# Six short vectors loaded as rows and spread by a product with ones, and the other small loads split over two semaphores

## What is computed

```
h = rms_norm(x, norm1_g)
proj = h @ w_in                                  # 1024 x 2856, read in six pieces
q = rms_norm(q, nsa_q_norm_g)                    # per head of 64
kc = rms_norm(silu(blocks(k_c) @ cmp_w1_k) @ cmp_w2_k, nsa_k_norm_g[0])
ks = rope(rms_norm(k_s, nsa_k_norm_g[1]));  kw = rope(rms_norm(k_w, nsa_k_norm_g[2]))
...                                              # attention branches, gated linear attention
o = rms_norm(o_gla, gla_norm_g) * silu(r)
x = x + concat(nsa, gla) @ w_out
logits = rms_norm(x, norm2_g) @ w_router + b_router
x = x + sum over the top 4 of 32 experts of gate * expert(x)   # w_gate_up, w_down: 32 x 12 MB
```

## Time and profile before

| | |
|---|---|
| median of 3 runs | 1162.44 us (1160.12 to 1165.05) |
| the profiled execution's own time | 1164.05 us |
| its span, first to last instruction | 1162.0 us |
| PE busy | 1083.2 us, 93% |
| DVE, ACT, POOL busy | 275.6, 129.9, 17.2 us |
| DMA moved | 426.37 MB, 367 GB/s on average |
| software DMA queue q0 | 752 packets, 1.32 MB, 1.3% of 16 engines' time |

### The profile page before, as it was taken

One profiled execution on the slowest core, in us unless ns is written; L12 is line 12 of the kernel. 1 busy time (PEld: TensorE's weight loads), 2 busy tenths in 40 slices (PEclk: granted clock), 3 DMA queues, 4 the chain that ended last, 5 costly groups with the idle time before them and its releaser, 6 DMA issues.

```text
span 1162.0 us, 13609 instructions
## 1 busy us (share of the span) xinstructions
PE 1083.2 (93%) x5502; PEld 485.6 (42%) x5502; DVE 275.6 (24%) x660; ACT 129.9 (11%) x290; POOL 17.2 (1%) x45
## 2 busy tenths in 40 slices
PE   7789999999999999999999999999999999999997
PEld 5354555444444443344333334334343433333442
DVE  1255442322222222222222111112222211221222
ACT  2224313000000000000000000000000000000001
POOL 5000000000000000000000000000000000000000
PEclk9889989999999999999999999999999999999999
DMA  9941253699999999999999999999999999999996
GB/s 210 336 157 73 73 218 144 259 399 418 418 418 418 418 419 418 418 417 417 418 417 418 417 418 417 419 417 418 417 418 418 417 418 418 418 418 419 418 418 277
DMA packets 83471, 426.37 MB, mean 367 GB/s; under 512 B 4752, under 2 KB 9968, under 8 KB 50656
## 3 DMA queue, kind: packets, MB, share of 16 engines
q1 hardware_dynamic: 82704, 424.85, 90.2%
q0 software_dynamic: 752, 1.32, 1.3%
HBM read 425.11 MB, written 1.05 MB: 367 GB/s over the span
## 4 chain that ended last, share of the span: by engine, by line
DMA 59%; PE 36%; DVE 2%; issue 1%; POOL 1%; ACT 1%; SPq 0%; DVEq 0%; POOLq 0%; ACTq 0%
DMA stage<-in_w_gate_up 54%; PE bank L1398 16%; PE bank L1407 5%; PE bank L1075 4%; PE bank L1388 3%; PE bank L1324 3%; DMA stage<-in_w_down 2%; DMA bdn<-in_b_down 2%; PE bank L1430 1%; PE bank L1091 1%; DMA stage<-in_w_in 1%; PE bank L1131 0%; PE bank L1114 0%; DVE pb L784 0%; PE bank L1422 0%
## 5 line engine op out<-in xcount | busy, mean ns | idle before, releaser
L1398 PE MATMUL bank<-stage,xs 128*64 128x512 f32 x2048 | 457.3, 596 | 48.5 <-DMA stage<-in_w_gate_up 46.8
L1398 PEld LDWEIGHTS bank<-stage,xs 128*64 128x64 f32 x2048 | 140.0, 137 | 360.7 <-issue 269.5
L1407 PE MATMUL bank<-stage,actf 128*64 128x512 f32 x1024 | 227.0, 595 | 1.2 <-DMA stage<-in_w_down 1.2
L992 DVE COPY gu<-bank 128x512 f32<-128x512 f32 x32 | 22.1, 692 | 450.2 <-PE bank L1398 450.2
L1388 PEld LDWEIGHTS bank<-onehot,xr 128*128 128x128 f32 x1024 | 116.8, 192 | 25.6 <-issue 25.6
L1407 PEld LDWEIGHTS bank<-stage,actf 128*64 128x64 f32 x1024 | 70.6, 137 | 132.4 <-issue 121.4
L1388 PE MATMUL bank<-onehot,xr 128*128 128x64 f32 x1024 | 121.0, 276 | 0.0
L1075 PE MATMUL bank<-stage,xt 128*128 128x512 f32 (+1 forms) x192 | 87.6, 610 | 0.9 <-DVE xt L685 0.9
L594 ACT COPY gu<-bank 128x512 f32<-128x512 f32 x32 | 18.8, 586 | 473.1 <-PE bank L1398 473.1
L1430 PE MATMUL bank<-ys,pgt 64*128 64x512 f32 x256 | 63.6, 615 | 1.0 <-ACT ys L598 1.0
L1014 DVE TENSOR_TENSOR pgr<-iota_f,posm 128x256 f32<-128x256 f32 x32 | 13.6, 425 | 188.2 <-PE bank L1415 188.2
(11 more groups left out here) (285 smaller groups left out, 430.3 us busy)
## 6 DMA issues: line engine op xcount, KB each, us to landing
stage<-in_w_gate_up SPq DMA_DIRECT2D x128, 2048.0 KB, 23.9
stage<-in_w_down SPq DMA_DIRECT2D x62, 2048.0 KB, 24.0
stage<-in_w_in SPq DMA_DIRECT2D x5, 2048.0 KB, 33.4
stage<-in_w_out SPq DMA_DIRECT2D x2, 2048.0 KB, 10.4
stage<-in_w_down SPq DMA_DIRECT2D x4, 1024.0 KB, 18.8
stage<-in_cmp_w_k SPq DMA_DIRECT2D x1, 2048.0 KB, 22.9
stage<-in_cmp_w_v SPq DMA_DIRECT2D x1, 2048.0 KB, 20.8
stage<-in_w_in SPq DMA_DIRECT2D x1, 1120.0 KB, 7.5
```

The costliest lines, as they stand in the source:

```text
L992: V.tensor_copy(gu[:, 1, :], up_banks[1][:]).then_inc(s["gu_lo"], 1)
L1398: last = mm(up_banks[a][b * CAP:(b + 1) * CAP, :], xs[:, k, :], w[:, kk, FF * a + 512 * b:FF * a + 512 * (b + 1)], start=k == 0, stop=k == ...
L1407: last = mm(down_bank[b * CAP:(b + 1) * CAP, :], actf[:, kk, j, :], w[:, kk, 512 * b:512 * (b + 1)], start=j == 0 and kk == 0, stop=j == D ...
```

## The change

The six broadcast loads (three into `g12`, one each into `gk0`, `glag` and `brt`) go. Four loads put the vectors behind each other into one row, `vecs`, of 416 numbers on partition 0. After `project(3)` PE multiplies a row of ones by it (`ones[0:1, :]`, 1 x 128, times 1 x 416), so that bank 3 holds the row in all 128 partitions. Six DVE instructions copy the parts to `g12`, `gk0`, `brt` and `glag`; the last also applies the factor 0.5 that `glag` had got in an instruction of its own. PE's next use of bank 3 waits for them (`gains`). `small` now counts ten loads: `wgate`, its bias, the positions, the four rows, `brow` and the two `posl`. The seven others (`w2`, `wrt`, `bdn`) come behind them and count on a new semaphore `late`, which DVE waits for ahead of the scaling of `wrt`, and PE ahead of `gated_bias` at 227 us. The memsets of `glrt` and `ones` move ahead of the loads on POOL, and ACT's copy into `glrt` waits for three of POOL's constants, not for all 20.

```diff
-N_SMALL = 19
+N_SMALL = 10
+N_LATE = 7
...
+            step(nc.gpsimd.memset(glrt[:], 1.0))
+            step(nc.gpsimd.memset(ones[:], 1.0))
             small = [
                 (wgate[0:RANK, :], gla_w_gate[0]),
                 (wgate[RANK:RANK + 1, :], gla_b_gate[0:1, :]),
                 (poss[:], positions[0].rearrange("(t p) -> p t", p=P)),
+                (vecs[:, 0:DH], nsa_q_norm_g[0:1, :]),
+                (vecs[:, DH:4 * DH], nsa_k_norm_g.rearrange("o b d -> o (b d)")),
+                (vecs[:, 4 * DH:4 * DH + DV], gla_norm_g[0:1, :]),
+                (vecs[:, 4 * DH + DV:], b_router[0:1, :]),
                 (brow[:], b_gate_up[0]),
                 (posl[:, 0, :], cmp_pos_k[0].rearrange("(c i) d -> c (i d)", i=2)),
                 (posl[:, 1, :], cmp_pos_v[0].rearrange("(c i) d -> c (i d)", i=2)),
-                (g12[:, 0:HQ, :], nsa_q_norm_g[0:1, :].partition_broadcast(P).to_broadcast([P, HQ, DH])),
-                (g12[:, HQ:HQ + 2, :], nsa_k_norm_g[0, 1:2, :].partition_broadcast(P).to_broadcast([P, 2, DH])),
-                (g12[:, HQ + 2:HQ + 4, :], nsa_k_norm_g[0, 2:3, :].partition_broadcast(P).to_broadcast([P, 2, DH])),
-                (gk0[:], nsa_k_norm_g[0, 0, :].partition_broadcast(NCW)),
-                (glag[:], gla_norm_g[0].partition_broadcast(P)),
+            ]
+            late = [
                 (w2[:, 0, :, :], split_k(cmp_w2_k[0])),
                 (w2[:, 1, :, :], split_k(cmp_w2_v[0])),
                 (wrt[:], split_k(w_router[0])),
-                (brt[:], b_router[0].partition_broadcast(P)),
             ] + [(bdn[r * E:(r + 1) * E, :], ...) for r in range(4)]
...
-            act.wait_ge(s["const"], N_CONST)
+            act.wait_ge(s["const"], 3)
             act.wait_ge(s["glrt_full"], 1)
...
+            dve.wait_ge(s["rows_full"], 1)
+            heads = banks[3][:, 0:4 * DH].rearrange("p (b d) -> p b d", d=DH)
+            V.tensor_copy(g12[:, 0:HQ, :], heads[:, 0:1, :].to_broadcast([P, HQ, DH]))
+            for b in range(2):
+                V.tensor_copy(g12[:, HQ + 2 * b:HQ + 2 * b + 2, :], heads[:, 2 + b:3 + b, :].to_broadcast([P, 2, DH]))
+            V.tensor_copy(gk0[:], banks[3][0:NCW, DH:2 * DH])
+            V.tensor_copy(brt[:], banks[3][:, 4 * DH + DV:4 * DH + DV + E])
+            V.tensor_scalar(glag[:], banks[3][:, 4 * DH:4 * DH + DV], 0.5, None, ALU.mult).then_inc(s["gains"], 1)
+            dve.wait_ge(s["gains"], 1)
             dve.wait_ge(s["small"], 16 * N_SMALL)
...
+            dve.wait_ge(s["late"], 16 * N_LATE)
             V.tensor_tensor(wrt[:], wrt[:], bc(gt2[:, DK:2 * DK], E), ALU.mult)
-            V.tensor_scalar(w2[:], w2[:], 0.5, None, ALU.mult)
-            link(V.tensor_scalar(glag[:], glag[:], 0.5, None, ALU.mult))
+            link(V.tensor_scalar(w2[:], w2[:], 0.5, None, ALU.mult))
...
             pe.wait_ge(s["small"], 16 * N_SMALL)
+            pe.wait_ge(s["const"], 4)
+            mm(banks[3][:, 0:4 * DH + DV + E], ones[0:1, :], vecs[:], start=True, stop=True).then_inc(s["rows_full"], 1)
...
             pe.wait_ge(s["proj"], 4)
+            pe.wait_ge(s["gains"], 1)
...
+            pe.wait_ge(s["late"], 16 * N_LATE)
             gated_bias()
```

More of the change, by code:

```diff
@@ L140, in decoder_layer @@
         g12 = sb("g12", [P, 12, DH])
+        vecs = sb("vecs", [1, 4 * DH + DV + E])
         gt = sb("gt", [P, NT, 24 + RANK])
@@ L215, in decoder_layer @@
             "xin0 xin1 grows g1_full g1t xt_full xt ms_x rsx proj_full proj small const act dve rope sin "
-            "glrw glrt_full glrt bias_full bias z_full absz e1 loga b_full bexp dec qd qdt_full qdt at_full ats "
+            "late rows_full gains glrw glrt_full glrt bias_full bias z_full absz e1 loga b_full bexp dec qd qdt_full qdt at_full ats "
             "u_full sta sgr grg o_full gsq glaout kx_full kx post_full post tb h_full sigh hid ht_full hidt "
@@ L370, in _ @@
                 (wrt[:], split_k(w_router[0])),
-                (brt[:], b_router[0].partition_broadcast(P)),
             ] + [(bdn[r * E:(r + 1) * E, :], b_down[0][:, 512 * (r % 2):512 * (r % 2) + 512]) for r in range(4)]
+            assert len(small) == N_SMALL and len(late) == N_LATE
             pool.wait_ge(s["stage0"], 16)
@@ L376, in _ @@
                 pool.dma_start(dst, src, allow_slow_non_contiguous=True).then_inc(s["small"], 16)
-            assert len(small) == N_SMALL
-            step(nc.gpsimd.memset(glrt[:], 1.0))
-            step(nc.gpsimd.memset(ones[:], 1.0))
+            for dst, src in late:
+                pool.dma_start(dst, src, allow_slow_non_contiguous=True).then_inc(s["late"], 16)
             step(nc.gpsimd.memset(tri[:], 1.0))
```

## The result

The changed kernel takes 1146.61 us (median of 4, 1146.35 to 1148.58), the kernel before in the same comparison 1163.74 us (median of 4). The ratio is 0.9858, 95% interval 0.9826 to 0.9890: 17.1 us faster, where 13.1 were forecast. The time lies 2.7 us under the 1149.3 that were forecast; the other 1.3 us of the difference are the kernel before, whose median was 1163.74 here and 1162.44 in the prediction. The profiled execution took 1148.58 us, the longest of the four, with a span of 1146.8 us, 15.2 less than before. What follows accounts for these 15.2 us, and the other 1.9 of the 17.1 are in no trace.

What follows compares the result with a forecast made beforehand. Expert-loop weight loads fill over half the span and start when the front ends, so the front's gain is the kernel's. 13.3 us at `hidden(8, 16)` less 0.2 slack gives 13.1; off the 1162.44 median, 1149.3 us, range 1146.5 to 1155.0.

Steps and rivals of the forecast that it cites:

- The two waits: Front, PE: 6.0 us behind `project(3)` for `bdn`, 3.94 us at `hidden(0, 8)` for `cmp_w1_v`; both late from slow broadcast packets.
- The stream: SP's loads in the front run 12.2 us earlier (13.4 + 1.3 - 2.5); `cmp_w1_v` lands at 55.9, not 68.1.
- the price of what stays: Front, software queue: the remaining 0.79 MB of small loads cost SP's stream 2.5 us.
- Which loads: Front, 19 to 29 us: the slow packets, 1.9 us each, are those of the broadcasts.
- PE's way: PE from `project(3)` to `hidden`: `project(4)` ends at 44.5, 9.0 us earlier; PE reaches `hidden` at 55.3.
- DVE's way: `norm_heads(1)` ends 16.1 us after `project(4)`, at 60.6; PE waits; `hidden(8, 16)` ends at 64.9, gain 13.3 us.
- from there on ... everything moves by as much: After `hidden(8, 16)`: no load is late, and everything moves by the same gain, 13.1 us after slack.
- D: Rival: PE's terms at their lower ends and clock up later in the front, another 2 us: 1147, chance 0.1.
- B: Rival: broadcasts cost only their bytes, the hole is the software queue's; no change, 1162.4, chance 0.07.
- C: Rival: the `late` loads hold DVE; slower, at 65 us it would cost 8 us, 1170; chance 0.02.
- A: Rival: `cmp_w1_v`'s load decides at `hidden(0, 8)`, not DVE; stream wins only 9 us; gain 9.1, 1153.3; chance 0.17.

Runs made afterwards that it cites:

- split_only: Kernel before with the second semaphore alone, broadcasts, w2, wrt and bdn counted on `late`, plus ACT's shorter wait for POOL's constants: 1162.79 us, ratio 0.9982.
- others_back: Changed kernel plus the five smaller broadcasts (all but the q gains') as loads that nothing reads, in their old places: 1149.90 us, ratio 0.9897.
- q_one_head: Kernel before with q gains spread by DMA once per partition, not eight times, DVE copying the other seven heads: 1149.51 us, ratio 0.9907.
- rows_one_sem: Changed kernel with all 17 small loads on one semaphore again, so the split is undone: 1147.10 us, ratio 0.9865.
- stall_only: rows_one_sem with the last small load issued only when `project(3)` is done, so PE stalls without the slow stream: 1159.26 us, ratio 0.9957.
- q_broadcast_back: Changed kernel plus the q gains' broadcast (256 KB, read by nothing), issued where it stood before and counted on `late`: 1156.66 us, ratio 0.9935.
- same_shape_apart: Changed kernel plus an unread load shaped and placed like the q gains' broadcast, but from 256 KB of different addresses: 1150.48 us.
- row2k_broadcast: Changed kernel plus an unread broadcast of one 2 KB row to 128 partitions, in the place of the q gains': 1148.62 us.
- hidden_whole: Changed kernel with both halves of `hidden` ahead of `heads_turned(1)`: 1145.17 us, ratio 0.9855.

## Why the prediction was right, and where it was off

**The two waits, and that they had one cause**: right. Removing the wait alone gave 1.5 us, putting the slow load back alone cost 10.0 us, and putting the stall back alone cost 12.2 (4.8 of them behind `heads_turned(1)`, in the stretch whose clock is looked at below). The last two add up to more than the 17.1 of both, so they overlap: the time in which PE stands for `small` is time in which `cmp_w1_v` comes nearer (split_only has the first wait no more, and PE stands 7.77 us for `cmp_w1_v` in place of 3.94).

**The stream.** Forecast 12.2 us earlier, `cmp_w1_v` at 55.9; measured 13.6 and 54.5. Right, and with it the price of what stays: from 16 to 41 us the windows carry 8.79 MB, which at 387 GB/s is 22.7 us of work in 25, so 2.3 us are lost where 2.5 were forecast.

**Which loads.** The prediction took the slow packets for those "of the broadcasts". Only the q gains' load is slow (others_back, q_one_head), and not for being a broadcast, but for reading its 256 bytes 1024 times. The sum did not depend on it, since all six went.

**PE's way.** `project(4)` was to end at 44.5 and ended at 47.3. Of the 2.8 us, 1.2 were lost ahead of all of it: the gains of the first norm landed 6.47 us after their issue, not 5, PE began to project at 11.57 instead of 10.15, and `project(3)` ended at 35.70 instead of 34.51. That is likely this execution's own: in the traces of the other kernels, where that load is the same, PE begins between 10.0 and 11.3. And 1.75 us were the clock: a stretch at 0.5 fell into `project(4)` (8.78 us for 7.03) though PE had no idle time ahead of it. The transposes took 0.97 us, not 1.4; the product with ones 0.89, not 0.7.

**DVE's way.** From the end of `project(4)` to that of `norm_heads(1)` 16.1 us were forecast, and it was 47.3 to 63.4. PE waited for it, as forecast. `hidden(8, 16)` ended at 67.68: a gain of 10.5 us there, not of 13.1 to 13.3, and all of the difference stems from the later end of `project(4)`.

**The step that was off by most** is the next one, "from there on ... everything moves by as much". From the end of `hidden(8, 16)` to the loop's first load it took 134.3 us before and 129.6 after, 4.7 us more gain. The windows of before and after, cut at about the same instructions (PEclk is the third number from the end):

```profile
78.20:140.00 61.80, 58.64 (x302) 31.36 (x303) 30.64 (x67) 23.63 (x82) 0.00 (x0) 1.00 0.19 68
140.00:161.00 21.00, 18.76 (x154) 12.21 (x152) 10.26 (x31) 7.08 (x16) 0.00 (x0) 0.84 0.39 148
161.00:195.00 34.00, 32.93 (x99) 16.39 (x99) 9.78 (x35) 7.64 (x17) 0.00 (x0) 0.95 0.35 142
195.00:212.00 17.00, 15.81 (x88) 10.51 (x89) 8.07 (x47) 2.37 (x4) 0.00 (x0) 0.90 0.36 152
```

```profile
67.70:129.50 61.80, 58.63 (x302) 31.34 (x303) 30.65 (x67) 23.66 (x82) 0.00 (x0) 1.00 0.19 68
129.50:148.00 18.50, 15.43 (x155) 10.65 (x153) 11.04 (x33) 7.66 (x17) 0.00 (x0) 1.00 0.49 187
148.00:182.00 34.00, 33.76 (x104) 16.90 (x104) 9.14 (x35) 7.30 (x16) 0.00 (x0) 0.95 0.35 138
182.00:197.00 15.00, 13.81 (x85) 9.22 (x85) 7.90 (x47) 2.13 (x3) 0.00 (x0) 1.00 0.38 158
```

The first stretch is 61.8 us in both, at a grant of 1.00. The second took 21.0 us at 0.84 and takes 18.5 at 1.00, the last 17.0 at 0.90 and 15.0 at 1.00; the third is 34.0 at 0.95 in both. The whole of it, from the end of `hidden(8, 16)` to the loop's first load, before and then after:

```profile
78.20:212.54 134.34, 126.68 (x642) 70.62 (x644) 58.75 (x179) 40.73 (x117) 0.00 (x0) 0.95 0.28 110
67.68:197.28 129.60, 121.94 (x642) 68.13 (x644) 58.74 (x179) 40.74 (x117) 0.00 (x0) 0.99 0.30 114
```

The same 642 PE instructions are busy for 4.74 us less, DVE and ACT for as long as before. The time at 0.5 in it is 13.6 us before (144.3 to 151.1, 161.3 to 164.7, 198.9 to 202.3) and 3.4 after (148.6 to 152.0); by an estimate half of the 10.2 us of difference, 5.1, is what a PE that is always busy would lose, and 4.7 is what it lost. So the mis-sized term is the clock: the forecast counted it only up to `hidden(0, 8)`, and only D had a price for it later on, 2 us. The mean grant over the span is 0.996 in all four runs of the changed kernel (0.994 to 0.997 in those of rows_one_sem) and 0.984 to 0.995 in the runs of the kernel before, and within that kernel the time goes with it (1160.15 us at 0.990, 1167.43 at 0.985; 1156.02 at 0.995). What brings a lapse at a given place I can't say: stall_only has them at the same instructions as before, q_broadcast_back has fewer and shorter ones, and a PE kept busy in the stall did not remove them. That part of the gain is measured, its cause is open.

**Luck.** The forecast of the whole is nearer than its parts. The gain up to `hidden(8, 16)` was 2.6 us smaller than forecast and the rest 4.7 us larger, for a reason that the forecast's sum did not have; the two offset each other in part, to 15.2 us for 13.1.

**The rivals.** B (the broadcasts cost what their bytes cost) fell: 256 KB from different addresses landed in 6.7 us from issue, as `brow` did in 6.1, and the q gains alone took 15.9 and held the stream meanwhile. C (`late` too late) did not come: the loads were there 13 us ahead of DVE. A (the load decides, not DVE) is what q_one_head shows in small: there PE stands 2.08 us for `cmp_w1_v`. D (1147) has the nearest time, and half of its mechanism came: the clock stayed up later on. PE's terms were not at their lower ends.

## What to carry over

A load that reads one short run into all partitions several times over (here 256 bytes, 128 times 8) can hold all DMA engines for microseconds, and every other load with it; read it once for each partition and let a compute engine make the copies. When a wait for a load ends late, look for the stretch in which the DMA share is high and the GB/s low, and at the time per packet in it, before taking the wait apart: the second semaphore alone was worth 1.5 us. And a moved front moves clock stretches: compare the granted clock over the same instructions before giving a gain to the edit's own steps.

## What the runs showed of the hardware that I had not expected

Reads of one address are quick up to a number and slow beyond it. 256 reads of one run of 256 bytes (each k gains' load), and 128 reads of a row of 2 KB, cost nothing visible; 1024 reads of one run of 256 bytes on the software queue hold the engines for about 10 us, at 76 GB/s in one load and at 123 and 64 in four (19 to 29 and 29 to 32 us). On the hardware queue such a load was slow too (22.9 us to land, 148 and 192 GB/s), but with short packets and idle engines, and whether by the same cause is open. Where between 256 and 1024 it begins wasn't tried. And the grant fell to 0.5 in `project(4)` of the changed kernel at 39.4 us, after 27.8 us in which PE had no gap; the traces of others_back, same_shape_apart, row2k_broadcast and hidden_whole, with the same work there, show 1.00 from 32 to 50 us.
